# A two-block transformer kernel: residual stream with features on partitions, norm factors multiplied into products

## What is computed

```
# first block, once
h = h + 0.5 * swiglu(rms_norm(h, norm_ffn1), w_ffn1_in, w_ffn1_out)      # FFN width 2816
h = h + merged @ w_out            # sliding attention + HGRN2 recurrence on rms_norm(h, norm_mix)
h = h + 0.5 * swiglu(rms_norm(h, norm_ffn2), w_ffn2_in, w_ffn2_out)
gate = sigmoid(rms_norm(h, norm_ple) @ w_ple_gate)
h = h + gate * (p @ w_ple_proj)
h = rms_norm(h, norm_final)
# second block, layer 0 and layer 1
h = h + mixer(rms_norm(h, attn_norm))       # 0: stick-breaking attention + RWKV7; 1: MLA
h = h + (gelu(causal_conv3(gate_in) + b) * u) @ ffn_w_out   # [u, gate_in] = rms_norm(h, ffn_norm) @ ffn_w_in
gate = sigmoid(rms_norm(h, ple_gate_norm) @ ple_w_gate)
h = h + gate * rms_norm(p @ ple_w_proj, ple_norm)
# rms_norm(x, g) = x * (mean(x*x) + 1e-6) ** -0.5 * g
```

## Time and profile before

| | us |
|---|---|
| median of 3 runs | 1626.96 (1626.9 to 1627.0) |
| span of the profiled execution | 1629.3 |
| TensorE busy | 1497.1 (92%) |
| TensorE weight loads busy | 1284.3 (79%) |
| VectorE busy | 704.1 (43%) |
| ScalarE busy | 550.6 (34%) |
| GpSimd busy | 549.9 (34%) |
| transfers | 223.24 MB, 137 GB/s on average |

### The profile page before, as it was taken

How to read it: one execution, slowest core, us unless ns; L and a number is a source line. 1 busy time by engine, 2 the same in 40 slices (tenths; PEclk the granted TensorE clock), 3 DMA queues, 4 the chain that set the end, 5 groups by cost and what they waited for, 6 DMA issues and landing times.

```text
span 1629.3 us, 21249 instructions
## 1 busy us (share of the span) xinstructions
PE 1497.1 (92%) x8792; PEld 1284.3 (79%) x8792; DVE 704.1 (43%) x885; ACT 550.6 (34%) x671; POOL 549.9 (34%) x209
## 2 busy tenths in 40 slices
PE   5999989999989999979979997999998888899996
PEld 4999978898668999668878855899967364899985
DVE  1545531353136454231564113566642171456654
ACT  3443310213124544321335111444342163444443
POOL 4655500031135554301021022546521044356541
PEclk9999989899999999989999768999999899999998
DMA  8555557332435555423400022455543402355540
GB/s 285 194 191 190 180 120 224 100 129 78 136 130 169 185 180 182 154 81 111 139 23 1 1 81 93 163 187 191 188 153 117 141 27 88 125 193 188 180 155 26
DMA packets 158212, 223.24 MB, mean 137 GB/s; under 512 B 5452, under 2 KB 135717, under 8 KB 158021
## 3 DMA queue, kind: packets, MB, share of 16 engines
q1 hardware_dynamic: 154284, 216.96, 40.4%
q10 hardware_dynamic: 3864, 5.38, 1.6%
HBM read 219.57 MB, written 2.62 MB: 136 GB/s over the span
## 4 chain that ended last, share of the span: by engine, by line
PE 85%; DVE 6%; ACT 4%; POOL 2%; issue 2%; DMA 0%; DVEq 0%; SPq 0%; POOLq 0%; ACTq 0%
PE ps L734 29%; PE ps L764 14%; PE ps L725 12%; PE ps L827 5%; PE ps L973 3%; PE ps L808 2%; PE ps L797 2%; PE ps L1098 1%; PE ps L958 1%; PE ps L1206 1%; PE ps L1222 1%; PE ps L890 1%; ACT weights_first_parts L1339 1%; PE ps L1093 1%; PE ps L1234 1%
## 5 line engine op out<-in xcount | busy, mean ns | idle before, releaser
L1689 POOL TENSOR_TENSOR weights_second_parts<-weight_bays,weights_first_parts 128x2048 fp32r<-128x2048 f32 x88 | 418.6, 4761 | 407.5 <-ACT weights_first_parts L1339 407.5
L1339 ACT ACTIVATE weights_first_parts<-weight_bays 128x2048 fp32r<-128x2048 f32 x132 | 249.8, 1909 | 174.9 <-PE ps L734 74.5
L734 PE MATMUL ps<-x_first_part,weights_first_parts 128*128 128x256 f32 x1408 | 199.0, 284 | 15.8 <-ACT x_first_part L1320 7.4
L725 PE MATMUL ps<-xT,weight_bays 128*128 128x256 f32 (+1 forms) x896 | 201.3, 386 | 2.6 <-DVE xT L1837 2.6
L734 PEld LDWEIGHTS ps<-x_first_part,weights_first_parts 128*128 128x128 f32 x1408 | 184.8, 192 | 21.2 <-issue 15.9
L734 PE MATMUL ps<-x_second_part,weights_first_parts 128*128 128x256 f32 x1408 | 201.3, 287 | 0.0
L734 PE MATMUL ps<-x_first_part,weights_second_parts 128*128 128x256 f32 x1408 | 198.5, 285 | 0.0
L725 PEld LDWEIGHTS ps<-xT,weight_bays 128*128 128x128 f32 (+1 forms) x896 | 171.5, 193 | 29.4 <-DVE xT L1837 3.3
L734 PEld LDWEIGHTS ps<-x_second_part,weights_first_parts 128*128 128x128 f32 x1408 | 184.9, 195 | 0.0
L734 PEld LDWEIGHTS ps<-x_first_part,weights_second_parts 128*128 128x128 f32 x1408 | 182.4, 193 | 0.0
L1863 DVE TENSOR_TENSOR hidden_second_part<-arena,hidden_first_part 128x512 fp32r<-128x512 f32 x44 | 117.9, 2679 | 42.4 <-ACT hidden_first_part L1329 42.4
(11 more groups left out here) (343 smaller groups left out, 1818.7 us busy)
## 6 DMA issues: line engine op xcount, KB each, us to landing
weight_bays<-in_w_ffn_in SPq DMA_DIRECT2D x44, 1024.0 KB, 5.1
weight_bays<-in_ffn_w_in SPq DMA_DIRECT2D x44, 1024.0 KB, 5.1
weight_bays<-in_w_ffn_out SPq DMA_DIRECT2D x22, 1024.0 KB, 4.9
weight_bays<-in_ffn_w_out SPq DMA_DIRECT2D x22, 1024.0 KB, 4.9
weight_bays<-in_w_in SPq DMA_DIRECT2D x19, 1024.0 KB, 5.4
weight_bays<-in_hyb_w_in SPq DMA_DIRECT2D x13, 1024.0 KB, 5.2
weight_bays<-in_ple_w_gate SPq DMA_DIRECT2D x8, 1024.0 KB, 4.9
weight_bays<-in_w_out SPq DMA_DIRECT2D x4, 1024.0 KB, 4.8
```

The source lines that it names most:

```text
L725: mm = nc.tensor.matmul(dst, lhs(k), xT[:, k] if rhs is None else rhs(k), start=(k == 0), stop=(k == n - 1), **kw)
L734: mm = nc.tensor.matmul(dst, w[:, k, j * P:(j + 1) * P], x[:, k], start=(n + k == 0), stop=(n == 2 and k == KD - 1))
L1339: nc.scalar.activation(hi, raw, ACT.Copy).then_inc(*w_hi_ready.inc(f, g, kind, of - g))
L1689: nc.gpsimd.tensor_tensor(lo, raw, hi, ALU.subtract).then_inc(*w_lo_g.inc(f, g, kind, of - g))
```

## The change

`h` is kept with features on partitions, eight tiles of 128x256. Then nothing has to be transposed between stages, and x is h times a gain, so that x_hi (ScalarE) and x_lo (VectorE, L1973) are made before the norm's factor is known. The factor is per token, and so a scale on the columns of every product: it is multiplied in where products leave PSUM.

- The sum of squares over features is taken by TensorE: ScalarE squares h, and 16 float32 products of one column (`add_squares`, L742) have a 128x128 square of them as their stationary side. VectorE makes mean and, after GpSimd's power, two diagonal matrices (`factors`, L1998), and two products of 128x128 with ones (`spread`, L758) put the 256 factors on all partitions; VectorE keeps them (`keep_factors`, L2003).
- In the FFN VectorE multiplies the gate and up products of each group by the factors (conv: L2057 in place of ScalarE's copy, L2058), and then works from SBUF alone.
- Out products of the FFN are 48 of 256 columns per group in place of 24 of 512 (L847); the gate of ple goes by feature columns, 192 of 256 columns in place of 96 of 512.
- The second parts of group 0's gate and up and of group 1's gate are VectorE's (L2025); from then on gate and up are GpSimd's (L1849), and its power comes ahead of them. In ple, GpSimd makes them in 4 pieces of 128x512 per chunk (L1866), all 4 chunks.
- The embedding products move (L770): those of ple1 into the start of mix1, those of ple20 and ple21 to the start of hyb and mla; their own sums, factors and scaling follow there.
- block1 isn't applied to h at once: two sums are taken, and gains and factors are combined.
- The input is transposed at the start (16 squares), and the output transposed back at the end, written by two queues.

The diff, cut to what the text speaks of:

```diff
-            def norm(n):
-                pe.wait_ge(*scaled_d.at(n, 0))
-                for k in range(KD):
-                    nc.tensor.transpose(ps[:, 4 + k // 2, (k % 2) * SEQ:(k % 2) * SEQ + P], hn[:, 0, k * P:(k + 1) * P], ident)
...
+            def add_pair(src, q, b):
+
+                for k in (2 * q, 2 * q + 1):
+                    for t in range(TT):
+                        mm = nc.tensor.matmul(ps[:, b, t:t + 1], src[:, k, t * P:(t + 1) * P], ones[:, 0:1],
+                                              start=(k + t == 0), stop=(k == KD - 1), skip_group_check=True)
+                return mm
+
+            def add_squares(n, src, b):
+
+                for q in range(PAIRS):
+                    pe.wait_ge(*squared.at(n, q))
+                    mm = add_pair(src, q, b)
+                mm.then_inc(*sums_p.inc(n))
+
+            def spread(n, b, factors=1):
+
+                pe.wait_ge(*diag_ready.at(n))
+                for c in range(factors):
+                    for t in range(TT):
+                        mm = nc.tensor.matmul(ps[:, b, c * SEQ + t * P:c * SEQ + (t + 1) * P], ones[:, 0:P], diag[:, 2 * c + t], start=True, stop=True)
...
+                    if g == 0:
+                        wait_split(pe, (w_hi_ready, w_lo_d), f, "gate", 0)
+                        through(first_features(f, [ps[:, 4 + j, 0:SEQ] for j in range(2)], *parts["gate"], False), gate)
+                        add_squares(f, sq, 6)
+                        wait_split(pe, (w_hi_ready, w_lo_d), f, "up", 0)
+                        split_features(ps[:, 4, SEQ:2 * SEQ], *parts["up"], 0)
+                        spread(f, 7)
+                        through(split_features(ps[:, 5, SEQ:2 * SEQ], *parts["up"], 1), up)
+                        return
...
-                    for t in range(TT):
-                        for half in range(2):
-                            for n, (x, w) in enumerate(((hid_hi, hi), (hid_lo, hi), (hid_hi, lo))):
-                                for j in range(2):
-                                    mm = nc.tensor.matmul(bank(2 * t + half), x[:, g % 2, j, t * P:(t + 1) * P],
-                                                          w[:, j, half * 512:(half + 1) * 512],
-                                                          start=(g == 0 and n + j == 0), stop=(g == GROUPS - 1 and n == 2 and j == 1))
...
+                    for tile in range(KD):
+                        for n, (w, x) in enumerate(((hi, hid_hi), (hi, hid_lo), (lo, hid_hi))):
+                            for j in range(2):
+                                mm = nc.tensor.matmul(ps[:, tile // 2, tile % 2 * SEQ:(tile % 2 + 1) * SEQ], w[:, j, tile * P:(tile + 1) * P],
+                                                      x[:, g % 2, j], start=(g == 0 and n + j + tile % 2 == 0),
+                                                      stop=(g == GROUPS - 1 and n == 2 and j == 1), skip_group_check=True)
...
+            def first_parts(n, q, gain):
+                act.wait_ge(*h_ready.at(n, q))
+                for k in (2 * q, 2 * q + 1):
+                    ins = nc.scalar.activation(x_hi[:, k], h[:, k], ACT.Copy, scale=col(gain, k))
+                ins.then_inc(*x_hi_a.inc(n, q))
+
+            def squares(n, q):
+                act.wait_ge(*h_ready.at(n, q))
+                nc.scalar.activation(sq[:, 2 * q:2 * q + 2], h[:, 2 * q:2 * q + 2], ACT.Square).then_inc(*squared.inc(n, q))
...
+            def second_parts(n, q, gain):
+                dve.wait_ge(*x_hi_a.at(n, q))
+                for k in (2 * q, 2 * q + 1):
+                    ins = v.scalar_tensor_tensor(x_lo[:, k], h[:, k], col(gain, k), x_hi[:, k], ALU.mult, ALU.subtract)
+                ins.then_inc(*x_lo_d.inc(n, q))
...
+            def factors(*n, b, at=0, slot=0):
+
+                dve.wait_ge(*sums_p.at(*n))
+                v.tensor_scalar(msq[:, at:at + 2], ps[:, b, 0:2], 1.0 / D, EPS, ALU.mult, ALU.add).then_inc(*mean_ready.inc(*n))
+                dve.wait_ge(*rstd_ready.at(*n))
                 for t in range(TT):
+                    ins = v.tensor_scalar(diag[:, slot + t], ident, rstd[:, at + t:at + t + 1], None, ALU.mult)
+                ins.then_inc(*diag_ready.inc(*n))
...
+            def keep_factors(*n, b, dst=rb):
+                dve.wait_ge(*spread_p.at(*n))
+                v.tensor_copy(dst[:], ps[:, b, 0:SEQ]).then_inc(*rb_ready.inc(*n))
...
+            def rest_of_weights(f, g, i=None, which=slice(0, None)):
+                for kind, of in split_steps(g)[which]:
+                    if g and kind != "out":
+                        continue
+                    raw, hi, lo = split_views(f, kind, of)
+                    dve.wait_ge(*w_hi_ready.at_group(i, f, g, kind, of - g))
+                    v.tensor_tensor(lo, raw, hi, ALU.subtract).then_inc(*w_lo_d.inc(f, g, kind, of - g))
...
                     if not conv:
-                        v.tensor_tensor(gluT[:, s], first, gatev[:, s], ALU.mult).then_inc(*conv_out.inc(f, g))
+                        v.tensor_tensor(gluT[:, s], first, by_token(rb[:]), ALU.mult).then_inc(*glu_in.inc(f, g))
+                        v.tensor_tensor(hidT[:, s], second, by_token(rb[:]), ALU.mult).then_inc(*glu_in.inc(f, g, "up"))
+                        dve.wait_ge(*gate_act.at_group(i, f, g))
+                        v.tensor_tensor(gluT[:, s], gluT[:, s], gatev[:, s], ALU.mult).then_inc(*conv_out.inc(f, g))
                         dve.wait_ge(*conv_out.at_group(i, f, g))
-                        v.tensor_tensor(hidT[:, s], gluT[:, s], second, ALU.mult).then_inc(*hid_ready.inc(f, g))
+                        dve.wait_ge(*glu_in.at_group(i, f, g, "up"))
+                        v.tensor_tensor(hidT[:, s], gluT[:, s], hidT[:, s], ALU.mult).then_inc(*hid_ready.inc(f, g))
...
+                    v.tensor_tensor(gpad[:, s, :, 2:2 + SEQ], second, by_token(rb[:]), ALU.mult).then_inc(*glu_in.inc(f, g))
+                    v.tensor_tensor(hidT[:, s], first, by_token(rb[:]), ALU.mult).then_inc(*glu_in.inc(f, g, "up"))
+                    dve.wait_ge(*glu_in.at_group(i, f, g))
...
-                    nc.gpsimd.tensor_tensor(lo, raw, hi, ALU.subtract).then_inc(*w_lo_g.inc(key))
+                    for c in range(4):
+                        part = slice(c * 512, (c + 1) * 512)
+                        ins = nc.gpsimd.tensor_tensor(lo[:, part], raw[:, part], hi[:, part], ALU.subtract)
+                    ins.then_inc(*w_lo_g.inc(key))
...
             def hyb():
-                norm("hyb")
-                pair_of_features(("wk", 0), 0)
+                pe.wait_ge(*rb_ready.at("ple1"))
+                embed("ple20", 1, 0, (0, 1))
+                add_squares("block1", sq, 4)
+                add_squares("hyb", sqg, 5)
+                embed("ple20", 1, 0, (2,))
+                spread("hyb", 6, 2)
+                embed("ple20", 1, 0, (3,))
+                embedding_kept(pe, "ple20", 0)
+                pair_of_features(("wk", 0), 0, first="hyb")
+                embedding_factors("ple20", 7)
+                embedding_kept(pe, "ple20", 1)
                 pair_of_features(("wk", 1), 1)
```

More of the change, by code:

```diff
@@ L671, in _ @@
                     group_load(n)
+            for half in range(2):
+                sp.wait_ge(*out_d.at(half))
+                sp.dma_start(out[0, P:2 * P, half * 512:(half + 1) * 512], outb[:, 1, half * 512:(half + 1) * 512]).then_inc(stored.sem, 16)
+            sp.wait_ge(stored.sem, 16 * 4)
         @block.tensor
@@ L947, in mix1 @@
                 pe.wait_ge(*att_d.at("merged", 3))
[L948 to L961 removed]
+                project_rows("mix_out", mT, "mix1")
@@ L1577, in mla @@
             def mla():
-                norm("mla", "attn_norm1")
+                arrive("mla")
+                embedding("ple21", 0, "ple_norm1")
                 act.wait_ge(*used_up_to(("down", 1)))
@@ L1614, in _ @@
             act.wait_ge(*cols_ready.at("first"))
+            for q in range(PAIRS):
+                first_parts("ffn1", q, "norm_ffn1")
             split_weights("ffn1", 0, which=slice(0, 1))
-            norm("ffn1", "norm_ffn1")
+            for q in range(PAIRS):
+                squares("ffn1", q)
             split_weights("ffn1", 0, which=slice(1, None))
             ffn("ffn1", False)
-            norm("mix1", "norm_mix")
+            for n in (1, 2):
+                act.wait_ge(*cols_turned.at("p", n))
+                nc.scalar.activation(pT[:, n].rearrange("p k s -> p (k s)"), ps[:, 5 + n], ACT.Copy).then_inc(*p_kept.inc(n))
+            arrive("mix1")
+            embedding("ple1", 4)
             bias_out()
@@ L1774, in mla @@
                     ins.then_inc(*mla_g.inc("probs", hd))
-            split_ffn("ffn1")
+            power("ffn1")
             pool.wait_ge(consts_in.sem, 16 * N_CONSTS)
@@ new lines, in arrive, with added, update @@
+            def arrive(n, update, gain=None):
+                for q in range(PAIRS):
```

(33 more changed lines are left out.)

674 lines of the change are left out of this document (376 added, 298 removed).

## The result

The changed kernel takes 1650.5 us (median of 4 runs, 1648.1 to 1652.7), the kernel before 1627.0 (median of 4 runs, 1626.9 to 1632.0). The ratio on record is 1.0125, with the interval 1.0103 to 1.0148; the two medians alone would give 1.0145. It is slower by 1.25%; forecast were 1645.5 us, 1.1% slower, range 1600 to 1666.

The account below looks back on a forecast made before the run. TensorE, busy 92% of 1629.3 us, was taken as the bound. Added 140.1 less removed 121.6 gave +18.5, a span of 1647.8, less 2.3 for runs: 1645.5 us; own range 1630 to 1660, whole range 1600 to 1666.

Parts of the forecast that it names:

- Sums: On TensorE, 13 sums of squares on the path, 32 rows of 0.109 us each: 3.5 us each, 45.5 us added.
- The low end (0.061): Low end for a row of a sum, from products with 64 stationary columns: 0.061 us a row, 20 us less.
- Clock: TensorE's clock falls to the 1.2 GHz level behind sums, 1.6 us a fall: 23.6 us added, ends 0 and 23.6.
- Rival 1: Whole kernel faster: the clock holds behind the sums and the shared port costs half; 1607.9 us, chance 0.33.
- Out products: FFN out products, 48 of 256 columns for 24 of 512: 0.17 us for each of 44 groups, 7.5 us added.
- Embeddings: Embedding products on TensorE, now in plain sight: 3 x 6.87 us, 20.6 us added.
- Start: At the program's start, TensorE's first product comes at about 18.0 and not 24.20: 6.2 us removed.
- Late second parts in ffn1 and ffn2: In ffn1 and ffn2, VectorE scales group 0's gate first (0.69 us) and second parts start later: 3.2 us added.
- Port: VectorE's SBUF-only instructions held by GpSimd at their shared port: 14.1 us in conv, 13.9 in ple, 28.0 us added.
- the late groups: In conv's late groups, taps and last product held by GpSimd: 3.0 us per conv, and 0.65 for the last group.
- Rival 2: In conv, slower still: VectorE and GpSimd set the loop; 1659 us if 5 groups are caught, 1696 if all; chance 0.13.
- restarts: TensorE's slow products after gaps, in mix1, FFN stages, hyb, ple, conv0 and conv1: 18.8 us removed.

Follow-up runs that it names:

- wide sums: Changed kernel with each sum's 16 one-column products made 8 of 256 columns, ones as stationary side: 1628.8 us, ratio 0.9983 to the kernel before.
- fp32r sums: Changed kernel with squares and ones written as fp32r, two columns per product of a sum: 1617.2 us, ratio 0.9920 to the kernel before.

## Why the prediction was right

**Bound and direction** were right: TensorE sets the end, the removed waiting time came back as TensorE's own work, and the chain shows it.

**Sums**, 13 x 3.5: measured 3.46 each at full clock, and two experiments fix the cause, rows of 0.108 with 128 stationary columns and of 0.058 with 64. The low end (0.061) was the wrong row for this shape, for the reason given. The floor of some 25 ns from start to start that the Trainium skill states ("TensorE: Matmul & The Clock Gate", on "Wait - 56ns, not 53.3ns?") did not come into play, as no row of a sum was under 0.058; the estimate of some 35 us less by it fell.

**Clock**, 23.6: about 22 by the wide sums, or near 29 before the 7.6 of waits that then appear. The forecast took one restart, 1.6 us, for nearly every sum; the two windows of conv0 hold 3.1 + 3.6 = 6.7 us at the lower level, and the sums' own rows run slower in it (4.44 and 8.64 in the chain for one and for two sums, 3.46 and 6.92 at full pace). Rival 1 rested on the clock staying up and fell with that experiment. The forecast had the clock fall behind all thirteen sums, and it did not. The chain right behind the two sums of embeddings, in hyb and in mla (full pace is 6.91):

```profile
730.20 8.70 PE ps L786 x32
...
1268.09 7.01 PE ps L1333 x32
```

In mla the clock stays at 1.00, and so it does behind the sum of ple20. ple1 and ple20 got the same edit: from the end of the out products of the FFN to the end of the gate products, ple1 went from 35.85 us to 36.95 at a mean granted clock of 0.86, ple20 from 35.99 to 30.50 at 1.00 (before, both with the embedding's 6.87 in them). Why the clock falls in one and not in the other no run here shows.

**Out products**, 7.5: 5.68 - 5.54 = 0.14 in 44 groups, 6.2. **Embeddings**, 6.87 each: 16 of the 32 rows take 3.45, as said. **Start**, 6.2: 5.0, the first product at 19.23 and not 18.0. **Late second parts in ffn1 and ffn2**, 3.2: TensorE's wait for GpSimd's there grew from 4.7 to 7.0, 2.3.

**Port**, 28.0, was the term that was off as a term of the sum. Its mechanism stands in each place it was named for (4.77 for the diagonals in conv, 2.5 in ple, x_second_part at 2.56 and 2.34 for two). But TensorE waited only 2.3 for diagonals, 5.5 for x and 4.5 for the hidden second part ahead of the last group of both conv stages, together 12.3 where 28 stood. For the diagonals the sum counted the fallen clock and the held VectorE as if they came one after the other; they lie beside each other, and only the longer counts. With the clock up, the diagonals alone cost 9.9 (wide sums) to 14.3 us (fp32r sums). That does not explain the rest: the waits for x and for the hidden second part are 5.5 to 5.7 and 4.4 to 4.5 in those two kernels as well. There VectorE is held as forecast and the price was too high (13.9 for ple, 7.3 for the late groups). No experiment took the wait for the hidden second part away; that it goes back to the port is read from the trace.

**Rival 2** did not come: a loop group of conv is 11.38 + 5.68 = 17.06 in the chain, before 16.95, all of it TensorE's.

The sum, +18.5, meets +16.9 by spans and +23.5 by medians. That it comes so near is in part luck. The port's 16 too many must be balanced by terms too small. Most of that is the clock: by the mean granted clocks, 0.951 before and 0.943 after, the time at the lower level grew from 160 to 188 us, and half of these 28, about 14, is lost (an estimate, as if TensorE were busy all that time), where the forecast had 23.6 added and 18.8 of restarts removed, net 4.8. The 5 or so by the wide sums are part of it. The start's 1.2 is another; the rest is not settled. The step from the span to the median was off as well: the forecast took 2.3 off the span, and the median lies 4.3 above it (1650.5 and 1646.2), since the profiled execution of the kernel before seems to have been a slower one of its kind, and that of the changed kernel was the fastest of four. This 6.6, less the 1.6 by which the span was forecast too long, is the whole miss of 5.0.

## What to carry over

A product of one column is not a cheap product. It costs the load of its stationary side, and it may take the clock of the dense work behind it; before moving a reduction to the bounding engine, price both, from rows with the same stationary shape, and ask whether half the rows (fp32r) or fewer stationary columns will do. Losses that lie beside each other don't add: removing the larger lays the smaller bare, and an edit that gains nothing alone can gain after it.

## What was not expected

- Halving the stationary side of the sums gave 33 us, 15 more than its rows (13 x 1.40), through the clock.
- Wide sums take TensorE as long as the narrow ones, and the kernel with them is 22 us faster: which side of a product is the stationary one was worth about as much as the whole change cost (23.5).
- A pause for an engine that is not the bottleneck (GpSimd waiting for x) moved a small instruction, its power, and gave back the gain.
